# Two attention layers of a DiT-like block: recurrence first, neighbourhood attention second, projection chunks between the pieces of both

## The reference, cut to what matters

```python
h  = rmsnorm_2(x,  norm1_g[l]) * (1.0 + sc1)  + sh1
hc = rmsnorm_2(xc, norm1_g[l]) * (1.0 + sc1c) + sh1c
p, pc = h @ w_in[l], hc @ w_in[l]     # q, k, v, o of the mLSTM; q, k, v of the attention; gates
y_m = head_layernorm(mlstm forwards + mlstm backwards, norm_g) * sigmoid(o)
y_n = neighborhood_attention(qn, kn, vn, qnc, knc, vnc, rpb)   # 8 x 16 window + 256 context keys
x = x + g1 * (concat(y_m, y_n) @ w_out[l])
x = x + g2 * sq_relu_mlp(rmsnorm_2(x, norm2_g[l]) * (1.0 + sc2) + sh2, w_mlp1[l], w_mlp2[l])
```

## Time and profile before

| what | us |
| --- | --- |
| median of 3 runs | 3753.07 |
| lowest, highest | 3747.66, 3754.51 |
| the profiled execution, its own time | 3749.57 |
| its span | 3747.8 |
| layer 0 of block 2, first projection to end of the output projection | 1763 to 2314 |
| layer 1 of block 2, the same | 2894 to 3365 |

### The profile page before, as it was taken

How to read it: one execution, slowest core, us unless ns; L and a number is a source line. 1 busy time by engine, 2 the same in 40 slices (tenths; PEclk the granted TensorE clock), 3 DMA queues, 4 the chain that set the end, 5 groups by cost and what they waited for, 6 DMA issues and landing times.

```text
span 3747.8 us, 50270 instructions
## 1 busy us (share of the span) xinstructions
PE 3521.9 (94%) x17570; PEld 2889.6 (77%) x17570; DVE 1556.2 (42%) x2490; ACT 1214.5 (32%) x1974; POOL 1743.3 (47%) x1972
## 2 busy tenths in 40 slices
PE   8999999999999999997989879999999979689998
PEld 6668888887668887786867777888887867577887
DVE  4533257775533257777045463211213044542112
ACT  3333332233333342223234432221222334323222
POOL 5225567786216567773322432333333322534554
PEclk9989999999999999997999858999998989779999
DMA  3102234442102234442211321111111211322222
GB/s 137 61 34 96 101 141 162 160 163 98 57 34 96 95 129 163 171 170 86 101 51 40 91 85 45 57 62 66 63 62 51 107 57 46 113 96 79 95 95 101
DMA packets 94036, 348.32 MB, mean 93 GB/s; under 512 B 10256, under 2 KB 10512, under 8 KB 92112
## 3 DMA queue, kind: packets, MB, share of 16 engines
q1 hardware_dynamic: 70416, 256.51, 19.4%
q10 hardware_dynamic: 23488, 90.02, 6.9%
HBM read 337.91 MB, written 8.59 MB: 92 GB/s over the span
## 4 chain that ended last, share of the span: by engine, by line
issue 39%; POOL 33%; PE 19%; DVE 5%; ACT 2%; DMA 1%; POOLq 0%; ACTq 0%; DVEq 0%; SPq 0%
POOL w_lo L471 32%; PE ps L825 3%; PE ps L827 3%; PE ps L826 3%; PE ps L1036 1%; PE ps L917 1%; PE ps L900 1%; PE ps L919 1%; PE ps L918 1%; DVE tiny L2099 1%; ACT sn L1428 1%; DMA m_row<-m_spill 1%; PE ps L1027 1%; ACT pn L1395 1%; DVE m_row L2132 0%
## 5 line engine op out<-in xcount | busy, mean ns | idle before, releaser
L471 POOL TENSOR_TENSOR w_lo<-w_raw,w_hi 128x256 fp32r<-128x256 f32 x1904 | 1648.2, 898 | 1845.4 <-ACT w_hi L1140 1832.7
L1140 ACT ACTIVATE w_hi<-w_raw 128x1024 fp32r<-128x1024 f32 x472 | 499.9, 1060 | 882.2 <-PE ps L827 446.1
L825 PE MATMUL ps<-c_hi,w_hi 128*128 128x512 f32 x1248 | 450.2, 361 | 34.1 <-DVE c_lo L1969 25.3
L826 PE MATMUL ps<-c_lo,w_hi 128*128 128x512 f32 x1248 | 446.3, 358 | 0.0
L827 PE MATMUL ps<-c_hi,w_lo 128*128 128x512 f32 x1248 | 443.0, 355 | 0.0
L546 PE MATMUL ps<-h_hi,w_hi 128*128 128x512 f32 x976 | 389.6, 399 | 0.0
L548 PE MATMUL ps<-h_hi,w_lo 128*128 128x512 f32 x976 | 383.6, 393 | 0.0
L547 PE MATMUL ps<-h_lo,w_hi 128*128 128x512 f32 x976 | 383.5, 393 | 0.0
L1887 DVE SCALAR_TENSOR_TENSOR ada_junk<-ada_w,c_silu 128x1024 f32<-128x1024 f32 x192 | 307.6, 1602 | 3.3
L825 PEld LDWEIGHTS ps<-c_hi,w_hi 128*128 128x128 f32 x1248 | 240.2, 192 | 85.6 <-DVE c_lo L1969 22.4
L826 PE MATMUL ps<-u_lo,w_hi 128*128 128x512 f32 (+1 forms) x768 | 273.4, 356 | 0.0
(11 more groups left out here) (330 smaller groups left out, 5918.2 us busy)
## 6 DMA issues: line engine op xcount, KB each, us to landing
w_raw<-in_w SPq DMA_DIRECT2D x476, 512.0 KB, 3.2
ada_w<-in_ada ACTq DMA_DIRECT2D x96, 512.0 KB, 5.5
m_row<-m_spill ACTq DMA_DIRECT2D x16, 768.0 KB, 6.5
wq_row<-wq_spill ACTq DMA_DIRECT2D x16, 384.0 KB, 5.3
x_spill<-x ACTq DMA_DIRECT2D x2, 2048.0 KB, 6.3
bias<-in_rpb ACTq DMA_DIRECT2D x8, 512.0 KB, 3.3
x<-x_spill ACTq DMA_DIRECT2D x2, 2048.0 KB, 8.4
c<-in_c SPq DMA_DIRECT2D x1, 2368.0 KB, 13.5
```

What stands on the lines that cost most here:

```text
L471: last = nc.gpsimd.tensor_tensor(w_lo[:, j, c], w_raw[:, j % RAW, c], w_hi[:, j, c].bitcast(F), ALU.subtract)
L825: nc.tensor.matmul(bank, w_hi[:, j, w], hi[:, part], start=(k == ends[0]), stop=False)
L826: nc.tensor.matmul(bank, w_hi[:, j, w], lo[:, part], start=False, stop=False)
L1140: nc.scalar.activation(w_hi[:, j, :], w_raw[:, j % RAW, :], ACT.Copy).then_inc(hi_ready, 1)
```

## The change

The weight stream of a layer is dealt anew: gates first, then the mLSTM's q, k, v and o by pair of heads, then the attention's q, k, v by pair of heads, and the three empty chunks last. On every engine the recurrence comes ahead of the attention. Six chunks are run before slot 0 of the recurrence, eleven between the pieces of its slots (`FILLS`), three after it, nine between the pieces of the attention's units; the last units (6 of 24 in layer 0, 4 of 16 in layer 1) have pieces of the first two output chunks between them instead. Units go by pair of heads, tokens and then context. The gate sums come right behind the first chunk. All projection chunks of the layer share one context bank (2) and two token banks (0 and 1), so the context half of a chunk waits until the chunk before has been read. `scores` of a unit moves ahead of the quarter, `weighted` behind it. `m_row` holds one slot instead of one pair (32 loads of half the size instead of 16), `wq_row` has two buffers, and its load for the next pair is issued a slot earlier. `om` becomes part of `km`, `yu` part of `qm`. The output projection walks banks `OUT_X`, `OUT_C`. The same matmuls, the same number of chunks.

```diff
+STREAM_2 = [("g", 0), ("q", 0), ("k", 0), ("v", 0), ("k", 1), ("v", 1), ("q", 1), ("k", 2), ("v", 2), ("q", 2), ("o", 0),
+            ("k", 3), ("v", 3), ("q", 3), ("o", 1), ("o", 2), ("o", 3)] \
+    + [(kind, hp) for hp in range(4) for kind in ("nq", "nk", "nv")] + [("pad", i) for i in range(3)]
...
+    rope_a = sb("rope_a", 9 * KB, [SEQ])
+    rope_b = sb("rope_b", 11 * KB, [SEQ])
+    wq_row = [sb("wq_row0", 15 * KB, [2, ALL]), sb("wq_row1", GATE + 4352, [2, ALL])]
+    hq = sb("hq", 21 * KB, [ST, 2, HEAD])
...
+        FILLS, TAIL, N_TILES = ((6, 7), (8,), (9, 10), (11,), (12, 13), (14,), (15,), (16,)), 17, 9
+        LOCAL = TAIL + 3
+        AT = {one: p for p, one in enumerate(STREAM_2)}
+        OUT_X, OUT_C = (0, 1, 3, 4, 0, 1, 3, 0), (2, 5, 6, 7, 2, 5, 6, 7)
...
+                def ahead(p):
+                    lower(g0 + p // RING, p % RING)
+                for p in range(RING, FILLS[0][0] + 2):
+                    ahead(p)
                 seen(0)
                 values(0)
+                ahead(FILLS[0][0] + 2)
                 seen(1)
-                lower(g, 2)
-                lower(g, 3)
...
+                for v in range(SLOTS):
+                    hp, f = v // 2, v % 2
+                    ahead(FILLS[v][0] + 3)
+                    if f == 0:
+                        if hp >= 1:
+                            level(hp - 1, 0)
+                            seen(v + 1)
+                        if hp + 1 < PAIRS:
+                            values(hp + 1)
+                    else:
+                        if v + 1 < SLOTS:
+                            seen(v + 1)
+                        if hp >= 1:
+                            level(hp - 1, 1)
+                    for p in FILLS[v][1:]:
+                        ahead(p + 3)
+                ahead(TAIL + 3)
                 level(PAIRS - 1, 0)
+                ahead(TAIL + 4)
                 level(PAIRS - 1, 1)
...
+                def parts(p, a):
+                    g, j, end = g0 + p // RING, p % RING, blocks(p)
+                    if a >= end:
+                        return
+                    if a == 0:
+                        pe.wait_ge(lo_ready, g * RING + j + 1)
+                        if p >= 2:
+                            pe.wait_ge(bank_read[(p - 2) % RING], g0 + (p - 2) // RING + 3)
+                    if a == KT and p >= 1:
+                        k = i % KT
+                        if p == 0 and i < KT:
+                            pe.wait_ge(hlo_ready, (FIRST_H + 2 * L) * KT + k + 1)
+                        w = slice(k * P, (k + 1) * P)
+                        part, bank = (X, ps[:, p % 2, :]) if i < KT else (C, ps[:, 2, 0:CTX])
...
+                for p in range(FILLS[0][0]):
+                    for q in range(blocks(p) // 4):
+                        parts(p, 4 * q)
+                        if q == 0 and p:
+                            finish(p - 1)
+                        if p == AT["k", 1] and q == 1:
+                            mlstm_keys(L, 0, roped)
+                    if p == AT["k", 1]:
+                        gate_columns_by_token(L)
+                    if p == AT["v", 1]:
+                        mlstm_additions(L, 0)
+                for v in range(SLOTS):
+                    hp, f = v // 2, v % 2
+                    quarters = [(p, q) for p in FILLS[v] for q in range(blocks(p) // 4)]
+                    n = len(quarters)
+                    second = max(1, n // 2 - 1)
+                    third = min(n - 1, second + max(1, n // 4))
+                    for i, (p, q) in enumerate(quarters):
+                        parts(p, 4 * q)
+                        if q == 0:
+                            finish(p - 1)
+                        if i == 0:
+                            mlstm_scores(L, v, first, roped)
+                        if i == second:
+                            mlstm_results(L, v, first)
+                            if f == 0 and hp >= 2:
+                                mlstm_by_feature(L, hp - 2, first)
+                            if f == 1 and hp + 1 < PAIRS:
+                                mlstm_keys(L, hp + 1, roped)
+                        if i == third and f == 1 and hp + 1 < PAIRS:
+                            mlstm_additions(L, hp + 1)
+                for p in range(TAIL, LOCAL):
+                    for q in range(blocks(p) // 4):
+                        parts(p, 4 * q)
+                        if q == 0:
+                            finish(p - 1)
+                        if p == TAIL and q == 0:
+                            mlstm_by_feature(L, PAIRS - 2, first)
+                        if p == LOCAL - 1 and q == 1:
+                            mlstm_by_feature(L, PAIRS - 1, first)
...
+                early = [(0, k, part) for k in range(4) for part in both] + [(1, k, X) for k in range(4)]
+                at = {place(u, need_ctx): u for u in range(len(units))}
...
-                for c in range(M_TILES):
+                for c in range(N_TILES):
                     for q in range(4):
                         u = at.get(4 * c + q)
+                        if u is not None and u + 1 < len(units):
+                            scores(u + 1)
...
                         if u is not None:
                             if u >= 1:
                                 weighted(u - 1)
-                            if u + 1 < len(units):
-                                scores(u + 1)
-                        parts(c, 4 * q, 4 * q + 4)
...
+                            finish(LOCAL + c - 1)
+                for i, u in enumerate(rest):
+                    if u + 1 < len(units):
+                        scores(u + 1)
+                    if i == 0:
+                        finish(LOCAL + N_TILES - 1)
+                    if i:
+                        share = early[(i - 1) * len(early) // (len(rest) - 1):i * len(early) // (len(rest) - 1)]
+                        for c, k, part in share:
+                            if k == 0:
+                                out_arrive(c)
+                                taken(("nk", 3), ("nv", 3))
+                            last = out_block(c, k, part)
+                            if (c, k, part) == early[0]:
+                                last.then_inc(chunk_used, 3)
+                    weighted(u - 1)
+                    by_key(u)
                 weighted(len(units) - 1)
-                finish(M_TILES - 1)
...
+            def mlstm_scores(L, v, first, roped):
+                hp, f, n, t0, c = slot(v, first)
+                roped(("q", hp), ("k", hp))
+                if v:
+                    pe.wait_ge(mg_ready, L * SLOTS + v)
+                if f == 0:
+                    pe.wait_ge(state_v, (L * PAIRS + hp + 1) * 10)
+                elif hp >= 2:
+                    pe.wait_ge(yu_ready, L * PAIRS + hp - 1)
...
+            def mlstm_results(L, v, first):
+                hp, f, n, t0, c = slot(v, first)
+                pe.wait_ge(qw_ready, L * SLOTS + v + 1)
+                if v:
+                    pe.wait_ge(post_v, (L * SLOTS + v) * 6)
+                else:
+                    pe.wait_ge(key_copied, L + 1)
...
+                    nc.scalar.activation(ym_hi[:, hp, first * P:ALL], qm[:, hp, first * P:ALL], ACT.Copy).then_inc(yhi_ready, 1)
+                split(g0, 0)
+                gate_rows(L)
+                act.wait_ge(spilled, (L + 1) * 32)
+                take(1)
+                take(2)
+                gate_rows_end(L)
+                take(3)
+                act.wait_ge(m_stored, (L + 1) * 32)
+                load_maxima(L, 0, first)
+                load_maxima(L, 1, first)
+                act.wait_ge(wq_stored, (L + 1) * 32)
+                load_query_weights(0)
...
                 for v in range(SLOTS):
                     hp, f = v // 2, v % 2
+                    take(FILLS[v][0] - 1)
                     if f == 0:
...
-                            weights(v + 1)
+                        if hp + 1 < PAIRS:
+                            if hp:
+                                act.wait_ge(qw_ready, L * SLOTS + 2 * hp)
+                            load_query_weights(hp + 1)
+                        for p in FILLS[v][1:]:
+                            take(p - 1)
+                        if hp >= 1:
+                            squares_of(hp - 1)
...
+                    else:
+                        if hp >= 1:
+                            deviation(hp - 1)
                         if hp + 1 < PAIRS:
                             keys_by_token(hp + 1)
-                            act.wait_ge(qw_ready, L * SLOTS + v + 2)
-                            load_query_weights(hp + 1)
+                    if v + 2 < SLOTS:
+                        act.wait_ge(mpv_ready, L * SLOTS + v + 1)
+                        load_maxima(L, v + 2, first)
+                    if v == SLOTS - 2:
+                        for i in range(2):
...
+                    if u == ending + 2:
+                        for j in range(1, RING):
```

(75 more changed lines are left out.)

778 lines of the change are left out of this document (350 added, 428 removed).

## The result

The changed kernel takes 3639.98 us (median of 4 runs, 3636.55 to 3644.45), against 3753.3 for the kernel before, run beside it: a ratio of 0.9702 with a 95% interval from 0.9685 to 0.9718. The forecast was 3647 and 3598 to 3706; the gain is 113.3 us where 106 were forecast. The execution that was profiled has a span of 3634.7 us.

The account below looks back on a forecast made before the run. PE, busy 94% of the span, was taken as the bound, so only its waits and low clock could give time: 201 us to win less 96 exposed left 105 off 3753.1, forecast as 3647, range 3598 to 3706.

Parts of the forecast that it names:

- The ceiling: Both layers: PE's content at full clock is 821 us against 1022, so 201 us is all there is to win.
- Slots: Recurrence slots: DVE's chain behind the scores outlasts the quarter, leaving 10 us exposed in each layer.
- Gates: Layer start: gate rows on DVE delay freeing chunk 2's bank, so PE waits at chunk 3: 5 / 8 us.
- Pads: Last units: three splits on ACT, the third waiting for a raw buffer with softmax behind it: 8 / 8 us.
- Hand-overs: Attention: weighted is behind a quarter, but layer 1 lacks a quarter in three query chunks: 3 / 8 us.
- Last units: Units with only scraps of output chunks: DVE's cycle of 5.5 us against 3.3 on PE, 10 / 8 us.
- Clock: Last units: PE under 60% busy there lowers its granted clock, costing 5 us in each layer.
- DVE beside POOL: Slots: DVE instructions lengthened beside POOL's, three a layer at 1.3 us, 4 us in each layer.
- full cover: Rival: slots and pads cost half and the clock holds, some 3602 us; chance 0.13.
- weights late: Slots, rival: POOL lowers later chunks' weights behind seen, which waits for an m_row load; 3779 us, chance 0.04.
- The old wait: Slots, rival: results wait as before, 20 us a layer instead of 10, 3667 us; within the forecast's range, no separate chance.
- the second rival: Slots: DVE and POOL serialise, three DVE instructions each behind a POOL instruction in 16 slots, 3701 us; chance 0.2.

Follow-up runs that it names:

- e12: Changed kernel with neighbourhood values copied first, gates' edit, splits spread, q_w at the slot's head, and results a quarter later in slots of four quarters: 3597.77 us, ratio 0.9592.
- e1: Changed kernel, but in seven of eight slots a layer scores stand behind the whole first chunk, with results and additions right behind them: 3737.97 us, ratio 0.9964.
- e4: Changed kernel, but DVE rotates chunk 2 ahead of the decay instructions, and a context half waits for the context bank's last user: 3646.3 us, ratio 0.9721.
- e5: Changed kernel, but the three splits stand one behind each of three successive units, not all behind one: 3633.9 us, ratio 0.9679.
- e3: Changed kernel, but ACT copies neighbourhood values to zn ahead of a unit's exponentials, not behind them: 3636.6 us, ratio 0.9696.
- the second execution: Changed kernel run and profiled once more, nothing edited: 3644.65 us in five runs, ratio 0.9717.
- e2: Changed kernel with one wq_row buffer, the next pair's load issued only after the pair's second slot used the row: 3646.33 us, ratio 0.9725.
- e11: Changed kernel with q_w at the head of the slot and results a quarter later where a slot has four quarters: 3630.1 us, ratio 0.9682.
- e6: Changed kernel, but DVE forms q_w at the head of the slot, ahead of the rotation: 3633.0 us, ratio 0.9682.
- e8: Changed kernel with neighbourhood values copied first, the gates' edit, the splits spread and q_w at the head of the slot: 3597.19 us, ratio 0.9587.

## Why the prediction was right, step by step

- **The ceiling.** 821 us of content against 1022. `e12` is at 864.6, so 44 us over it, and the changed kernel, at 911.9 by the same marks, 91 over it; nothing shows the content wrong.
- **Slots.** Forecast 17.5 and 24 us; slot 1 took 17.9, slot 0 23.4. Exposed 10 and 10, measured 7.2 and 4.6 of waits. The mechanism was right (DVE behind the scores, one quarter of cover), its size a little too large. The chain ends in `qm`, not in the waits of about 1 us for `weigh` that I named as the sign. What I did not see is how steep the other side is. I priced the bare chain at 27 us a layer as the bound; `e1` shows 48 a layer (95 / 2) on top of what the changed kernel waits, because the clock goes with it.
- **Gates.** Forecast 5 and 8 for one wait for a bank that DVE frees: 3.7 in layer 0, and in layer 1 two waits of 3.7 and 2.0 (the third of the line's 6.2 us, 0.5, is in slot 0). The place was right, as `e4` shows, the size 1 to 2 us too large.
- **Pads.** Forecast 8 and 8 on ACT's wait for a raw chunk: 5.34 on ACT, 6.7 and 4.5 on PE, and 7.9 and 7.2 by `e5`, clock included. Right.
- **Hand-overs, 3 and 8.** The term that failed. Layer 0 has 9.3 us of waits for `zn` (11.2 by `e3`), layer 1 0.6. I looked for missing quarters on PE and put the loss in layer 1; the loss comes from the order of ACT, where the copy stands behind a softmax that DVE holds up. The copy stands behind a pair's first unit in both layers. In layer 1 PE has the scores of that unit earlier (at 3103.2, where the chunk is done at 3109.5, against 2106.9 and 2109.7 in layer 0), and DVE has added the mask before them (3099.6 to 3100.9) and not behind the context unit before (2108.9 to 2110.2).
- **Last units, 10 and 8.** 4.9 and 4.8 us of waits for `pn` and `sn`: half.
- **Clock, 5 and 5.** About right for the last units, where I put it, and left out elsewhere. From the third wait for `zn` on, the last units of layer 0 ran at 0.84, and those of layer 1 at 0.86, which is 5.6 and 3.3 us at most (windows below). The 148.3 us of units ahead of that in layer 0, with the waits for `zn` in them, ran at 0.97, 4.4 us more. And the recurrence at 0.98 and 0.95 has its own share, 3.6 and 7.5 at most, and 9.5 at 0.95 in the second execution. I had put its clock at 1.0.

```profile
2167.80:2202.80 35.00, 24.25 (x176) 17.51 (x174) 12.84 (x29) 17.18 (x34) 8.29 (x12) 0.84 0.29 96
3190.00:3213.80 23.80, 15.48 (x115) 11.78 (x116) 7.35 (x15) 10.80 (x17) 8.35 (x12) 0.86 0.38 139
```

- **DVE beside POOL, 4 and 4.** Next section: 16.4 us on DVE, hidden but for the waits for `qm`.
- **Loads.** `m_row` cost nothing beyond its issue; `wq_row`'s second buffer was given the credit for a wait that the new order removes without it (`e2`).

The sum of what was exposed came to 45 forecast and 52.7 measured in layer 0 (505.7 - 453), 51 and 39.8 in layer 1 (407.8 - 368): two errors of opposite sign. PE's waits, those for `c_lo` left out, come to 31.8 and 21.5 us, and the lower clock in the recurrence and the units to at most 13.6 and 10.8; the rest of the two sums, some 7 us each, isn't resolved. And 4.6 us of the gain were the first block's, where I had said that the rest of the kernel would stay within 2 us. A forecast within 7 us is partly luck: the two errors nearly cancel, and the first block adds its share. Of the rivals, full cover (3602) is what the kernel reaches with four edits more. Its sum was wrong as it stood: half of slots and pads (18) and the clock (10) taken off 96 leave 68 exposed and not 50, so 3620. The second is dealt with below. As for the others, weights late (3779) never showed: no wait for `w_lo` in a slot. The old wait (3667) is out by the 7.2 and 4.6, where it needed 20 a layer.

## What to carry to other kernels

Work of another stage in a dependent chain pays twice, by covering the waits and by keeping TensorE's clock up, so put a piece between every two links and not ahead of the chain: the same chunks in the same slots, ahead of the chain, lost 98 of 113 us. When work is interleaved on one engine, read the order of the others: a copy queued behind another stage's wait is where the new gap opens. And when a kernel's clock hangs on short waits, judge an edit by its own stretch, and take the kernel's profile twice, before a median of a few runs condemns it. Then put the edits together: only several of them at once were clear of the spread here.

## What the runs showed of the hardware

**Short waits move the clock, and not the same way each time.** Same code, same waits up to the last slots: 181.7 us at 0.98 and 189.5 at 0.95. Five waits of 0.9 to 2.3 us in a stretch of 180 went with a clock of 0.90 to 0.98 in the seven executions with this order of slots, and the stretch took 181.7 to 197.1 us. With 2.8 us of waits left it was 1.00 in `e11` and 0.98 in `e12`, with 3.0 it was 0.95 in `e6` and with 3.3 it was 0.98 in `e8`. What in a given execution decides it stays open.

**DVE and POOL.** `q_w` and `qm` take 0.55 us alone (0.42 in layer 1). In the 16 slots they took 31.9 us in place of 15.5. The ends line up, start and length in us:

```profile
1965.14 1.78 POOL L532 TENSOR_TENSOR hs<-hs,cols 128x768 f32<-128x768 f32 x1
```

```profile
1965.51 1.82 DVE L2226 TENSOR_TENSOR qm<-qm,wq_row 128x384 f32<-128x384 f32 x1
```

POOL ends at 1966.92 and `qm`, begun 0.37 us behind POOL, 0.41 later: it did its own 0.55 us of work nearly whole after POOL was done. That is what the Trainium skill (SBUF — State Buffer, Who interferes with whom) states, and what the second rival was built on. The trace has it throughout: 31 of the 32 `q_w` and `qm` began while a POOL `TENSOR_TENSOR` ran, and each of them ended 0.41 or 0.42 us behind that instruction in layer 0 and 0.28 in layer 1, whatever was left of it (0.17 to 1.44 us). So a hit costs what is left of POOL's instruction less 0.14 us. The rule holds and the rival's time (3701) did not come: for `qm` the cost was mostly 0.8 us in layer 0 and 0.5 in layer 1 and not 1.3, and 24 of the 32 lost more than 0.1 us, where 48 hits were priced (16 of them on the rotation's sum, which isn't among the 32). The rival's sign, `q_w` over 1 us in most slots, showed in 3 of 16; `qm` was over 1 us in 9. What it cost PE in waits is within the 11.8 us for `qm`; a quarter of PE's work covered the rest.
